# Layer norms of the last block, the tile ahead of them and the first slices behind them, in two halves of the tokens

## What is computed

```
def layer_norm(x, g, b):
    xf = x.astype(jnp.float32)
    mu = jnp.mean(xf, -1, keepdims=True)
    var = jnp.mean(jnp.square(xf - mu), -1, keepdims=True)
    return ((xf - mu) * lax.rsqrt(var + EPS_2) * g + b).astype(x.dtype)

def swiglu_half(x, w1, w3, w2):
    return 0.5 * ((jax.nn.silu(x @ w1) * (x @ w3)) @ w2)
...
    for l in range(DEPTH):
        x = layer_norm(ALPHA * x + swiglu_half(x, ffn1_w1[l], ffn1_w3[l], ffn1_w2[l]), ln1_g[l], ln1_b[l])
        h = x @ w_in[l]
        ...
        mix = jnp.concatenate([out_a, out_b, out_c], axis=-1) @ w_out[l]
        x = layer_norm(ALPHA * x + mix, ln2_g[l], ln2_b[l])
        x = layer_norm(ALPHA * x + swiglu_half(x, ffn2_w1[l], ffn2_w3[l], ffn2_w2[l]), ln3_g[l], ln3_b[l])
```

## Time and profile before

| what | value |
|---|---|
| time, median of 3 runs | 3958.81 us (3958.09 to 3960.32) |
| the profiled execution's own time | 3959.48 us |
| its span | 3957.70 us |
| PE busy | 95% |
| DVE busy | 53% |
| ACT busy | 35% |
| chain that ended last | PE 88%, DVE 6%, ACT 5%, issue 1% |

### The profile page before, as it was taken

How to read it: one execution, slowest core, us unless ns; L and a number is a source line. 1 busy time by engine, 2 the same in 40 slices (tenths; PEclk the granted TensorE clock), 3 DMA queues, 4 the chain that set the end, 5 groups by cost and what they waited for, 6 DMA issues and landing times.

```text
span 3957.7 us, 44541 instructions
## 1 busy us (share of the span) xinstructions
PE 3756.9 (95%) x18460; PEld 3115.7 (79%) x18460; DVE 2090.5 (53%) x3697; ACT 1390.9 (35%) x2106; POOL 86.4 (2%) x164
## 2 busy tenths in 40 slices
PE   8998989999999999999999978999999999799998
PEld 5985569999986688888887766888788877577886
DVE  5936767644456543333337477433633374765335
ACT  4434542211365432322226533222322256333222
POOL 0100001111000000000000000000000000000000
PEclk9998999999999999999999958999999999789999
DMA  6410004333220122232222201222222222012222
GB/s 222 151 50 6 17 27 136 123 128 128 99 70 22 43 93 99 96 109 96 99 97 77 85 6 43 94 98 96 88 96 96 96 85 80 22 34 85 99 98 80
DMA packets 92884, 333.33 MB, mean 84 GB/s; under 512 B 11364, under 2 KB 11532, under 8 KB 92428
## 3 DMA queue, kind: packets, MB, share of 16 engines
q1 hardware_dynamic: 77040, 278.10, 20.2%
q0 software_dynamic: 12800, 41.95, 3.4%
q10 hardware_dynamic: 2844, 10.44, 0.7%
HBM read 328.35 MB, written 2.10 MB: 83 GB/s over the span
## 4 chain that ended last, share of the span: by engine, by line
PE 88%; DVE 6%; ACT 5%; issue 1%; DMA 0%; DVEq 0%; ACTq 0%; SPq 0%
PE PS L513 73%; PE PS L1085 2%; PE PS L515 2%; PE PS L1103 1%; PE PS L1073 1%; PE PS L1604 1%; PE PS L1070 1%; PE PS L1438 1%; PE PS L2477 0%; PE PS L946 0%; PE PS L718 0%; PE PS L1409 0%; PE PS L2106 0%; DVE H_r L682 0%; ACT ring_hi L373 0%
## 5 line engine op out<-in xcount | busy, mean ns | idle before, releaser
L513 PE MATMUL PS<-arena_r,ring_hi 128*128 128x512 f32 (+1 forms) x6160 | 2082.3, 377 | 78.1 <-DVE H_r L682 70.7
L513 PE MATMUL PS<-arena_r,ring_r 128*128 128x512 f32 (+1 forms) x4688 | 1758.2, 375 | 0.0
L513 PEld LDWEIGHTS PS<-arena_r,ring_hi 128*128 128x128 f32 x6160 | 1155.2, 189 | 260.8 <-DVE H_r L682 62.1
L513 PE MATMUL PS<-H_r,ring_hi 128*128 128x512 f32 (+1 forms) x3216 | 1208.7, 376 | 0.0
L513 PEld LDWEIGHTS PS<-arena_r,ring_r 128*128 128x128 f32 x4688 | 884.9, 189 | 131.9
L382 DVE TENSOR_TENSOR ring_r<-ring,ring_hi 128x1024 fp32r<-128x1024 f32 x514 | 627.3, 1222 | 651.3 <-ACT ring_hi L373 650.8
L373 ACT ACTIVATE ring_hi<-ring 128x1024 fp32r<-128x1024 f32 x514 | 541.6, 1055 | 869.9 <-DMA ring<-weights_dram 862.2
L513 PEld LDWEIGHTS PS<-H_r,ring_hi 128*128 128x128 f32 x3216 | 609.7, 190 | 95.4 <-issue 3.1
L1737 ACT ACTIVATE arena<-PS 128x512 f32<-128x512 f32 x88 | 52.6, 598 | 533.5 <-PE PS L513 533.5
L1245 DVE SCALAR_TENSOR_TENSOR XH<-PS,mods,XH 128x256 f32<-128x256 f32 (+1 forms) x168 | 79.4, 517 | 235.3 <-PE PS L513 219.3
L344 DVE CAST arena_r<-arena 128x512 fp32r<-128x512 f32 (+1 forms) x184 | 74.3, 404 | 199.2 <-ACT arena L1292 196.1
(11 more groups left out here) (378 smaller groups left out, 3207.6 us busy)
## 6 DMA issues: line engine op xcount, KB each, us to landing
ring<-weights_dram SPq DMA_DIRECT2D x526, 512.0 KB, 3.2
rstd<-ada_later_dram POOLq DMA_DIRECT2D x54, 256.0 KB, 2.9
mean<-ada_later_dram POOLq DMA_DIRECT2D x53, 256.0 KB, 3.0
ada_extra<-ada_later_dram POOLq DMA_DIRECT2D x53, 256.0 KB, 3.0
XH<-xT_dram ACTq DMA_DIRECT2D x1, 3072.0 KB, 20.6
ring<-weights_dram ACTq DMA_DIRECT2D x4, 512.0 KB, 3.8
out_dram<-XH SPq DMA_DIRECT2D x8, 256.0 KB, 2.0
con<-second_dram ACTq DMA_DIRECT2D x1, 1536.0 KB
```

The lines of the kernel that those rows point to most:

```text
L513: ins = pe.matmul(PS[:, o.bank, 0:hi - lo], w[:, 0, :], x, **flags)
```

## The change

Two halves of the tokens, `HALVES` (columns 256 to 512 and 512 to 768), are treated apart at five of the six norms (`add_norm_halves`; the last norm stays as it is, and so do the first block's norms).

- The last output tile (m = 7) of the GEMM ahead has two PSUM banks of its own, 2 and 3, one for each half (`tail_pe`). PE runs all slices for the first half, then all for the second. In an FFN, after slice 8 of the second half, in the mixer behind it, come the sums of the first half and one of the second (`tail_sums_first_pe`).
- Statistics, roots, and tiles 0 to 2 of the norm go for the first half, then for the second (`norm_halves_dve`, `norm_halves_act`). Tiles 3 to 7 go whole, with ACT instead of DVE writing their high part.
- The first unit's slices 0 to 2 (`HALF_K` = 3) run for the first half of the columns, then for the second (`first_slices_pe`), with the remaining sums of the second half behind slice 0 of the first. Slices 3 to 7 are whole. The weights of those slices are given back in the second pass.
- To keep banks 2 and 3 free, the other seven tiles of that GEMM turn over four banks instead of six, and so do the first four of an FFN.

```diff
+        def tail_sums_first_pe(pe, t):
+            (oa, ob), (a, b) = t["outs"], (half_cols(*seg) for seg in HALVES)
+            pe.wait_ge(part_sum.sem, part_sum.next("pe"))
+            pe.wait_ge(first_used.sem, first_used.next("pe"))
+            pe.matmul(PS[:, 1, 0:256], C("ones"), scratch[:, a], start=True, stop=False)
+            pe.wait_ge(tile_acc.sem, tile_acc.next("pe", KD - 2))
+            pe.matmul(PS[:, 0, 0:256], C("ones"), sq_buf(t, 0, *LAT[0])[:, a], start=True, stop=False)
+            pe.wait_ge(evac["dve"].sem, oa.freed)
+            pe.matmul(PS[:, 1, 0:256], C("ones"), X[:, t["m"], HALVES[0][0]:HALVES[0][1]], start=False, stop=True).then_inc(sum_ready.sem, 1)
+            pe.wait_ge(tile_sq.sem, tile_sq.next("pe", KD))
+            pe.matmul(PS[:, 0, 0:256], C("ones"), sq_buf(t, t["m"], *LAT[0])[:, a], start=False, stop=True).then_inc(sum_ready.sem, 1)
+            pe.matmul(PS[:, oa.bank, 0:256], C("ones"), scratch[:, b], start=True, stop=False)
...
+        def tail_pe(pe, t):
+            kt, weights = t["kt"], []
+            for half, (o, (lo, hi)) in enumerate(zip(t["outs"], t["segs"])):
+                for k in range(kt):
...
+                    if half == 1 and k == min(kt - 1, 8):
+                        tail_sums_first_pe(pe, t)
+        def first_slices_pe(pe, unit):
+            weights = {}
+            for half, (lo, hi) in enumerate(HALVES):
+                for k in range(HALF_K):
+                    pe.wait_ge(xlo_ready.sem, unit[0]["halves"][k, half])
...
+                    if half == 0 and k == 0:
+                        tail_sums_second_pe(pe, unit[0]["behind"])
...
+        def norm_halves_act(act, t, eps, affine):
...
+            square(*HALVES[0])
+            roots(*HALVES[0])
+            for k in range(HALF_K):
+                scale(k, *HALVES[0])
+            square(*HALVES[1])
+            nc.scalar.activation(small[:, 159:160], V("one"), ACT.Ln)
+            roots(*HALVES[1])
+            for k in range(HALF_K):
+                scale(k, *HALVES[1])
+            high_up_to(act, Splits.high + 1)
+            for k in range(HALF_K, KD):
+                (lo, hi), = LAT
+                scale(k, lo, hi)
+                affine(act, k, lo, hi, out=xhi(True, k, lo, hi)).then_inc(xhi_by_act.sem, 1)
+                if k == 4:
+                    high_up_to(act, Splits.high + 1)
...
+            finish(oa, *first)
+            statistics(1, 0, *first)
+            for k in range(HALF_K):
+                ins = centre(k, *first)
+            v_link(dve, ins)
+            split_up_to(dve, t["last_slab"] + 3)
+            dve.wait_ge(std_ready.sem, std_ready.next("dve"))
+            for k in range(HALF_K):
+                times_root(k, *first)
+            split(0, *first)
+            finish(ob, *second)
+            split(1, *first)
+            split(2, *first)
+            statistics(oa.bank, ob.bank, *second)
+            for k in range(HALF_K):
+                centre(k, *second)
+            v_link(dve, centre(HALF_K, *whole))
+            dve.wait_ge(std_ready.sem, std_ready.next("dve"))
...
-            add_norm(LAT, "eps2", True, layer_norm_affine("ln1", l))
+            add_norm_halves("eps2", layer_norm_affine("ln1", l))
...
-            add_norm(LAT, "eps2", True, layer_norm_affine("ln2", l))
-            add_gemm(ffn_plans(l))
-            add_norm(LAT, "eps2", True, layer_norm_affine("ln3", l), last=(l == 1))
+            add_norm_halves("eps2", layer_norm_affine("ln2", l))
+            add_gemm(ffn_plans(l, tail=(l == 0)))
```

More of the change, by code:

```diff
@@ L221, in __init__, with take @@
         self.first = 0
-    def take(self, who):
-        bank = self.first + self.n % (8 - self.first)
+    def take(self, who, bank=None):
+        if bank is None:
+            bank = self.first + self.n % (8 - self.first)
         self.n += 1
@@ new lines, in tail_sums_second_pe @@
+        def tail_sums_second_pe(pe, t):
+            (oa, ob), b = t["outs"], half_cols(*HALVES[1])
+            pe.wait_ge(evac["dve"].sem, ob.freed)
+            pe.matmul(PS[:, oa.bank, 0:256], C("ones"), X[:, t["m"], HALVES[1][0]:HALVES[1][1]], start=False, stop=True).then_inc(sum_ready.sem, 1)
+            pe.matmul(PS[:, ob.bank, 0:256], C("ones"), sq_buf(t, 0, *LAT[0])[:, b], start=True, stop=False)
+            pe.wait_ge(tile_sq.sem, tile_sq.next("pe"))
+            pe.matmul(PS[:, ob.bank, 0:256], C("ones"), sq_buf(t, t["m"], *LAT[0])[:, b], start=False, stop=True).then_inc(sum_ready.sem, 1)
@@ L496, in gemm_pe @@
                 kt = unit[0]["kt"]
-                for k in range(kt):
+                if "tail" in unit[0]:
+                    tail_pe(pe, unit[0])
+                    continue
+                if "halves" in unit[0]:
+                    first_slices_pe(pe, unit)
+                for k in range(HALF_K if "halves" in unit[0] else 0, kt):
                     if k in unit[0].get("beside_pe_at", {}):
@@ L524, in gemm_pe @@
                     unit[-1]["beside_pe"](pe)
-            if "sums" in tiles[-1]:
+            if "sums" in tiles[-1] and "tail" not in tiles[-1]:
                 row_sums_pe(pe, tiles[-1])
@@ L614, in gemm_evac @@
                     squares_act(eng, t)
+                if who == "dve" and "tail" in t:
+                    sums_ahead_dve(eng, t)
+                    continue
                 if who == "dve":
@@ L643, in planned, with ftile, last_in_halves @@
             return (Planned.at - 1) // SLAB
-        def ftile(rhs, segs, who, ev, kt=KD, post=None, late=None):
-            return dict(mode="F", n=1, kt=kt, segs=segs, rhs=rhs, ev=ev, post=post, late=late, outs=[banks.take(who) for _ in segs],
-                        last_slab=planned(kt))
+        def ftile(rhs, segs, who, ev, kt=KD, post=None, late=None, own=None):
+            return dict(mode="F", n=1, kt=kt, segs=segs, rhs=rhs, ev=ev, post=post, late=late,
+                        outs=[banks.take(who, own[i] if own else None) for i in range(len(segs))], last_slab=planned(kt))
+        def last_in_halves(m):
+            return dict(segs=HALVES, own=(2, 3)) if m == KD - 1 else dict(segs=LAT)
         def ttile(rhs, toks, n, who, ev):
@@ L667, in program @@
             need, at, ahead = [], 0, 0
+            halves, behind, last = {}, None, None
         def split_tiles_of(segs, first=0):
@@ L1736, in ffn_plans @@
                 for m in range(n):
+                    banks.first = 4 if q == 0 and m < 2 else 2
                     a = ftile(x_x, LAT, "act", lambda eng, ps, lo, hi, m=m: nc.scalar.activation(h[:, m, :], ps, ACT.Silu))
@@ L2020, in mix_plan @@
             banks.first = 4
-            tiles = with_sums([ftile(lambda k, lo, hi: x_x(MIX_ORDER[k], lo, hi), LAT, "dve", ev_for(m)) for m in range(KD)], "mean")
+            tiles = with_sums([ftile(lambda k, lo, hi: x_x(MIX_ORDER[k], lo, hi), who="dve", ev=ev_for(m), **last_in_halves(m)) for m in range(KD)], "mean")
+            tiles[-1]["tail"] = True
             banks.first = 0
@@ L2643, in add_gemm @@
             tiles[0]["input_ready"] = (xlo_ready, Fresh.need)
+            if Fresh.behind:
+                tiles[0]["halves"], tiles[0]["behind"] = Fresh.halves, Fresh.behind
+            Fresh.behind, Fresh.last = None, tiles[-1]
             def act_fn(e):
@@ L2661, in add_norm, with add_norm_halves @@
             split_tiles_of(segs)
+        def add_norm_halves(eps, affine):
+            t = Fresh.last
+            Norms.affine += KD + HALF_K
+            add(None, lambda e: norm_halves_act(e, t, eps, affine), lambda e: norm_halves_dve(e, t), barrier=False)
+            Fresh.halves, Fresh.behind = {(k, half): Fresh.at + HALF_K * half + k + 1 for half in range(2) for k in range(HALF_K)}, t
+            Fresh.at += 2 * HALF_K
+            Fresh.need = [None] * HALF_K + [Fresh.at + k + 1 for k in range(KD - HALF_K)]
+            Fresh.at += KD - HALF_K
         def add_split(src, second, segs, first=0):
```

120 lines of the change are left out of this document (113 added, 7 removed).

## The result

The changed kernel takes **3975.89 us** (median of 5 runs, 3974.43 to 3979.59) against 3959.30 (3958.09 to 3960.76, 5 runs) for the kernel before on the same chip: ratio 1.0046, 95% interval 1.0035 to 1.0057. It is slower by 16.6 us. The forecast was 3969, slower, with a range up to 3975. So the direction came out and the size did not: the median lies 0.9 us above the range. The profiled execution was the longest of its five, 3979.59 us with a span of 3977.8, 20.1 over the span of the kernel before.

What follows compares the result with a forecast made beforehand. PE, busy 95% of the span, bounds the kernel, so only its idle waits can be won. 3959.5 - 2.7 (halves) + 13.0 (clock) + 0.4 (banks) = 3970.2, 3969.5 at the median's level, taken as 3969; range 3955 to 3975.

Steps and rivals of the forecast that it cites:

- Prices of halves and the chain: DVE, ACT and PE step times at 256 columns; PE restarts 5.81 us after the statistics, where it was 7.73.
- rival E: DVE falls behind around the restart and whole slices wait too; 3976 us and more; chance 0.05.
- Ahead of the statistics: Last output tile in halves brings statistics earlier: 1.41 us per FFN norm, 0.81 per mixer norm, 5.8 in all.
- Behind the statistics, without the clock: From statistics through the first unit, 31.9 us against 31.3 before: 0.6 lost per norm, 3.1 over five.
- The clock: PE falls to 1.2 GHz behind both waits: five first falls at 1.4, four second at 1.5, +13.0 us.
- The bound of 17.5: Upper bound of the clock cost: both costs at all five norms, the first at 2.0 us each.
- The banks: In two FFNs the fifth up tile waits for the third's Silu, 0.2 us each: +0.4 us.
- A: The forecast itself: both waits at each norm cost clock; 3964 to 3975 us; chance 0.55.
- B: The second wait at the norms mostly passes without a clock fall; 3960 to 3966 us; chance 0.22.
- C: Not slower: clock lost no more often or longer than before, decided at the first restart; 3955 to 3959; chance 0.13.
- D: Split works as meant: PE idles under 5 us per norm, no low clock, over 7.9 us won; chance 0.05.

Runs made afterwards that it cites:

- Filled kernels: Discarded matmuls put on PE in the norms' waits: kernel before with its five waits filled, 3954.03 us; changed kernel with both waits filled, 3957.97 us.
- the banks' turn: Kernel before with the change's turn of PSUM banks alone, four instead of six: 3956.99 us, ratio 0.9998.

## Why the prediction was wrong in size

**Prices of halves and the chain: right.** The last tile's 60 matmuls of 256 columns take 7.19 us (forecast 7.20). First waits are 4.34 and 5.05 us (forecast about 4.4 and 5.1), second ones 2.46 (forecast 2.5) in all five norms. From statistics to restart it is 5.88 (5.81). No slice from 3 on waits, so rival E fell.

**Ahead of the statistics: right, a little small.** 1.58 and 0.98 per norm instead of 1.41 and 0.81, 6.7 us instead of 5.8. The 0.2 until DVE sees the sums was too long: it is 0.02 in the chain, 2098.18 to 2098.20.

**Behind the statistics, without the clock: small.** The sum had 31.9 us beside 29.5 at full clock, 2.4 a norm. Filled kernels show 13.4 / 5 = 2.7. Less the clock share that the kernel before pays (9.1; the forecast had 9.0), it is +4.3 us where the sum had +3.1. Whole change at full clock against the kernel before, the banks left out: -6.7 + 4.3 = -2.4 us (forecast -2.7).

**The clock: the mechanism right, the term too small.** This is the step that failed at the norms: "5 x 1.4 + 4 x 1.5 = +13.0 us" measured 15.8. The number of second falls was five of five, in every profile of the changed kernel, and not four: 7.1 us at 1.4 each, where the forecast had 6.0. The first falls cost 8.8, where it had 7.0. Their delay of the second statistics was priced right (7.3). What it left out is that the sums behind the second mean sum still run at the low level, so that DVE, with its first two steps done, waits again for the square sum: 1.5 us over three norms. It also took the fall as coming 3.5 to 5.1 us after PE stops. The latest of the five in its own trace comes after 4.9 (a granted clock of 0.98 over 5.07 us in the earlier trace rows leaves 0.2 us at the low level), and in the changed kernel the level falls between 2.0 and 5.0 us after, in four norms within the wait and in one (ln3 of layer 0) 0.7 us behind the restart. The bound of 17.5 held the value. Choosing four of five rested on three short waits in one execution. The one of 3.23 us, without a fall there, has one in the changed kernel, and the one of 1.96 us, with a fall there, has none in the two other executions of the same program. Such a count of three was too thin for any number between none and all. In the changed kernel each second wait comes some 8 us after PE resumed at the low level, and the run with the first wait filled says that this may matter: same length of wait, three falls of five.

**The banks** cost 0.7 instead of 0.4: both waits are there, 0.36 us each. Norms and banks in all: -6.7 + 4.3 + 15.8 + 0.7 = 14.1 us where the sum had 10.7.

**Outside the norms: a term that the sum didn't have.** It took every stage that the edit leaves alone at no change, with the clock that it had. One fall that is new and one that is longer, behind the 3.2 us waits at the mixers' beginnings, go with 3.1 us; why they come is open. The account of the miss: 3.4 us too few at the norms and 3.4 in the mixers make 6.8 of the 6.9 between 3969 and 3975.9. That it closes so well is in part luck: executions of one kernel differ by up to 6 us, in the mixers and ahead of the first norm. The upper end of the range came from a count of the clock at the norms alone; with the mixers' 3 us it would have held the time.

**Of the rivals**, A held with both falls; its reason "both waits cost clock" is shown by taking them away one at a time and together. B fell: no second wait passes in the changed kernel. Two of five do with the first wait filled, but there the first falls are gone too, so its 3959.06 us isn't B's price. C would have needed PE at full clock soon after the restart. D wanted no low clock at all and PE idle for under 5 us per norm. It is idle for 7.1 (35.4 / 5), and even where filling keeps the clock up the changed kernel is no faster than the kernel before (0.9997). By the time alone the result could pass for E's (3976 and more), but E's sign, waits in slices 3 to 7, isn't there.

The Trainium skill ("TensorE: Matmul & The Clock Gate", A second HAM failure mode) tells of another kernel that micro-idles between groups of matmuls make the clock oscillate. The traces of the changed kernel agree: idle 4.34, low for 3.1 to 4.8 us of work, full, idle 2.46, low for 3.4. With the first wait filled the second idle has that effect in three norms of five only. The forecast had weighed it at four falls in five.

## What to carry to other kernels

A wait of TensorE costs its length and then the low clock behind it, here 0.42 to 0.46 us for each of some 3 to 5 us of work: cutting one wait in two shorter ones can pay for that twice, and a split has to be counted in falls as well as in idle time. When a wait can't be shortened, give PE matmuls that nobody reads until about a microsecond before its input comes; that took a handful of lines, and with nine waits filled it won 14.0 us, more than any term of this change. And a stage that the edit doesn't touch isn't at no change for that: the same wait of 3.2 us kept its clock in one program and lost it in the other.

## What the runs showed of the hardware

- Whether a wait of 2.46 us is followed by 1.2 GHz isn't a matter of its length alone. Behind a low stretch it was in 20 of 20 cases (four profiles of the changed kernel), behind filled waits in three of five. Nor is it fixed by the program: the wait of 1.96 us at 1325 had the low level behind it in one profile of the kernel before and in none of the two others, the one of 2.18 us at 1733 in three of four of the changed kernel. A rest of 0.63 to 0.91 us was never followed by a fall at a norm (five cases in the kernel before filled, ten in the changed one filled).
- The level need not fall within the wait: the one of 2.46 us from 2112.16 is at 1.00 throughout, and the 0.50 begins near 2115.7, a microsecond behind the restart. In the mixer norms it begins 0.3 us behind it (2481.0 after 2480.70).
- The wait of 3.23 us ahead of the mixer in layer 0: no low level behind it in four profiles (the kernel before three times, the banks' turn once), 2.9 to 6.2 us of work at the low level in the other ten.
- A stretch at 0.50 behind a second wait lasts 3.3 to 3.4 us of PE work in each of five norms, though different matmuls lie in it.
- The mixers run largely at 0.50 in every kernel (148 to 204 us of PE work from 1700 us on outside the norms). Their time doesn't follow that number: 628.5 us with 193.6 in the kernel before with five waits filled, 624.7 with 187.5 in the one with nine, 624.5 with 152.9 in the one with the banks' turn. So the price of 0.42 to 0.46 holds where PE sets the pace, as behind the norms, and was measured nowhere else.
